# Who copies the transposed attention weights out of PSUM: ScalarE for both heads, or VectorE for the first and ScalarE for the second

## The reference, cut to what matters

```python
z = q @ k.T * scale                       # 128 queries against kv_len keys, per head
log_keep = where(mask, log_sigmoid(-z), 0)
after = cumsum(log_keep, reverse=True) - log_keep
attn = where(mask, exp(log_sigmoid(z) + after), 0)
out = attn @ v
```

## Time and profile before

| | |
|---|---|
| time, median of 3 executions | 1342.16 us (1341.47 to 1343.16) |
| the profiled execution | 1342.95 us, of which its span is 1341.2 us |
| TensorE busy | 1242.6 us, 93% of the span |
| VectorE busy | 468.9 us, 35% |
| ScalarE busy | 381.1 us, 28% |
| GpSimd busy | 121.0 us, 9% |
| mean granted TensorE clock | 0.969 of full speed |

### The profile page before, as it was taken

The page is one execution under the profiler, slowest core; times in us unless marked ns, Lnnn a source line. Parts: engine busy times, 40 slices in busy tenths (PEclk is TensorE's granted clock), DMA queues, the critical chain, the costliest instruction groups (busy, mean ns, idle before and its releaser), DMA issues.

```text
span 1341.2 us, 23288 instructions
## 1 busy us (share of the span) xinstructions
PE 1242.6 (93%) x9734; PEld 602.4 (45%) x9734; DVE 468.9 (35%) x833; ACT 381.1 (28%) x571; POOL 121.0 (9%) x206
## 2 busy tenths in 40 slices
PE   7999999999989999998999956999999999999980
PEld 3444444444557777775445532333333333333320
DVE  3035301244357777774364353111111111111117
ACT  1034402333145565555222122111111111111114
POOL 1000000000021221220000001010101010101010
PEclk9999999999989999999999977999999999999995
DMA  5110001010000001001704019776799499397226
GB/s 220 32 47 31 32 32 47 32 31 16 0 2 3 34 4 34 4 3 65 267 6 157 28 44 354 275 273 197 268 313 312 148 319 367 101 369 254 55 38 259
DMA packets 61013, 170.19 MB, mean 127 GB/s; under 512 B 3184, under 2 KB 3312, under 8 KB 60928
## 3 DMA queue, kind: packets, MB, share of 16 engines
q1 hardware_dynamic: 54384, 145.31, 29.0%
q0 software_dynamic: 6544, 23.63, 7.4%
HBM read 144.29 MB, written 24.64 MB: 126 GB/s over the span
## 4 chain that ended last, share of the span: by engine, by line
PE 84%; DVE 6%; DMA 4%; ACT 3%; issue 2%; POOL 0%; SPq 0%; POOLq 0%; DVEq 0%; ACTq 0%
PE PS L1829 31%; PE PS L205 19%; PE PS L1300 8%; PE PS L214 3%; PE PS L659 3%; PE PS L994 2%; PE PS L678 2%; PE PS L1003 2%; PE PS L1013 2%; PE PS L1822 2%; DMA YT<-x1d,RK 1%; PE PS L348 1%; PE PS L1440 1%; PE PS L734 1%; DMA XS<-in_xT 1%
## 5 line engine op out<-in xcount | busy, mean ns | idle before, releaser
L205 PE MATMUL PS<-XS 128*128 128x512 f32 x672 | 293.9, 597 | 7.6 <-DMA XS<-in_xT 7.1
L1829 PE MATMUL PS<-XS,YT 128*64 128x512 f32 x656 | 287.9, 596 | 3.5 <-DMA SQ<-in_w_upx 2.6
L1829 PE MATMUL PS<-SQ,YT 128*64 128x512 f32 x488 | 216.4, 597 | 0.0
L1829 PE MATMUL PS<-RK,YT 128*64 128x512 f32 x672 | 211.1, 593 | 0.0
L205 PEld LDWEIGHTS PS<-XS 128*128 128x128 f32 x672 | 127.1, 191 | 172.7 <-issue 163.9
L1829 PEld LDWEIGHTS PS<-XS,YT 128*64 128x64 f32 x656 | 88.9, 137 | 185.4 <-issue 180.8
L1300 PE MATMUL PS<-SQ,YT 128*128 128x512 f32 x256 | 114.0, 594 | 0.6 <-issue 0.6
L1917 DVE TENSOR_TENSOR YT<-YT,PS 128x256 f32<-128x256 f32 x42 | 15.8, 418 | 274.7 <-PE PS L1829 274.7
L1829 PEld LDWEIGHTS PS<-RK,YT 128*64 128x64 f32 x672 | 65.9, 137 | 74.7 <-issue 74.7
L1300 PEld LDWEIGHTS PS<-SQ,YT 128*128 128x128 f32 x256 | 47.7, 190 | 56.7 <-issue 56.5
L1829 PEld LDWEIGHTS PS<-SQ,YT 128*64 128x64 f32 x488 | 66.4, 138 | 0.0
(11 more groups left out here) (386 smaller groups left out, 1591.2 us busy)
## 6 DMA issues: line engine op xcount, KB each, us to landing
RK<-in_w_down SPq DMA_DIRECT2D x6, 2048.0 KB, 12.6
XS<-in_w_in SPq DMA_DIRECT2D x21, 512.0 KB, 3.3
XS<-in_w_gate SPq DMA_DIRECT2D x5, 2048.0 KB
XS<-in_w_upx SPq DMA_DIRECT2D x5, 2048.0 KB
XS<-in_w_down SPq DMA_DIRECT2D x5, 2048.0 KB
RK<-in_w_gate SPq DMA_DIRECT2D x5, 2048.0 KB, 19.7
SQ<-in_w_gate SPq DMA_DIRECT2D x4, 2048.0 KB
RK<-in_w_upx SPq DMA_DIRECT2D x4, 2048.0 KB, 19.7
```

The lines of the kernel that those rows point to most:

```text
L205: m = e.matmul(acc[:, half * HB:(half + 1) * HB], XS[:, 8 + n % 4, kt * P:(kt + 1) * P], XS[:, kt, half * HB:(half + 1) * HB], start=kt == ...
L1829: ins = e.matmul(acc[r, :], rows[:, r], third_cols(n, k, at, HB), start=start, stop=stop)
```

## The change

`sba_turned` no longer takes its copy operation from the engine but as an argument. ScalarE calls it in step 2 only, for the second head, and VectorE calls it in step 0, for the first head. Waits, semaphore, source and destination stay as they were.

```diff
-        def sba_turned(e, u, hh):
+        def sba_turned(e, copy, u, hh):
 
             if 0 <= u < NU:
                 w = SPANS[u][4] - SPANS[u][3]
                 wait(e, s_bx, 2 * u + hh + 1)
                 wait(e, s_bv, u - 1)
-                e.copy(AT2[u % 2][:, hh, 0:w], PS[1][:, 0:w]).then_inc(s_bt, 1)
+                copy(AT2[u % 2][:, hh, 0:w], PS[1][:, 0:w]).then_inc(s_bt, 1)
 
         def sba_act(e, j):
             step = j % KINDS
-            if step in (0, 2):
-                sba_turned(e, j // KINDS - 2, step // 2)
+            if step == 2:
+                sba_turned(e, e.copy, j // KINDS - 2, 1)
...
         def sba_dve(e, j):
             step = j % KINDS
+            if step == 0:
+                sba_turned(e, e.tensor_copy, j // KINDS - 2, 0)
```

## The result

| | kernel before | kernel after |
|---|---|---|
| median of 20 executions each, on one chip | 1343.05 us | 1344.91 us |
| lowest and highest | 1337.41 and 1344.25 | 1343.07 and 1348.43 |
| profiled execution, of it the span | 1342.95 us, 1341.2 | 1343.07 us, 1341.3 |
| mean granted TensorE clock | 0.969 | 0.972 |

The times' ratio is 1.0021, with a 95% interval of 1.0012 to 1.0029. The medians lie 1.9 us apart. The ratio over 1, times 1342 us, is 2.8 us, and its interval runs from 1.6 to 3.9. So the kernel is slower by an amount at the edge of what I had called no change (0.2%, 2.7 us). The forecast was 1344.2 us.

What follows compares the result with a forecast made beforehand. TensorE was taken to bound the mixer stage. VectorE's copies, hold less slack place by place, cost 1.97 us, rounded 2.0, and ScalarE's relief gains 0: 1344.2 us against the median of 1342.16, range 1341.0 to 1349.8.

Steps and rivals of the forecast that it cites:

- What bounds the stage: Mixer stage: TensorE sets the pace, busy 236.51 of 250 us; only its 13.5 us of idle time can change.
- The relief at 0: ScalarE's queue: losing 36 copies, 17.5 us of work, gains TensorE 0, at most a single 0.3 us wait.
- What a copy holds up: VectorE's queue: each copy delays the rest by 0.61 us for 512 columns, down to 0.20 for 128; 17.1 us in all.
- place C of block 0: Block 0, 512-column copy: step-2 transposes and the weights L1083 slip, costing 0.60 us for both together.
- place A of block 1: Block 1, 384-column copy: hold 0.48 us less slack 0.05 ahead of TensorE's L659, costing 0.43 us.
- place A of block 4: Block 4, 256-column copy: U ends with slack 0.06 us ahead of TensorE's L659, costing 0.28 us.
- D of block 6: Block 6, 512-column copy: U slips by 0.28 us against slack 0.17 ahead of L774, costing 0.11 us.
- the three small ones: Places in blocks 5, 2 and 3, each under 0.1 us, taken together as 0.15 us.
- the 27: The other copy places, costed at nothing: VectorE idles afterwards for TensorE anyway, or TensorE needs the result later.
- The sum: Mixer stage: hold less slack over the charged places, 1.97 us, rounded to 2.0 us slower.
- The stages behind: Stages behind the mixer: of the same length, so the 2.0 us is expected at the end too.
- VectorE late as a rule: Rival, mixer stage: VectorE's extra 17.1 us makes it late from place to place; 7.6 us slower, 1349.8 us; chance 0.22.

Runs made afterwards that it cites:

- e5: Kernel after, with ScalarE given a dummy copy of the same width in step 0 at 35 of 36 places: 1345.13 us, ratio 1.0025 to the kernel before.
- e4: Kernel before, with ScalarE's first-head copy cut to 8 columns, so the attention's output differs: 1320.84 us, ratio 0.9832.
- e6: Kernel before, with ScalarE's second sigmoid L1049 moved behind its copy L816 in c3 and c9: 1336.62 us against 1341.27, ratio 0.9958.
- e2: Kernel before, with VectorE copying first heads only in the nine spans where the prediction charged a cost: 1344.01 us, ratio 1.0014.
- e1: Kernel before, with VectorE copying first heads only in the 27 spans costed at nothing: 1342.20 us against 1342.12, ratio 1.0001.
- e3: Kernel after, with VectorE copying each first head twice in 35 spans, once into an unused part of TT: 1354.87 us, ratio 1.0101 to the kernel before.
- e7: Kernel after, with ScalarE's second sigmoid L1049 moved behind its copy L816: 1342.90 us, ratio 1.0009 to the kernel before.
- e10: Kernel after, profiled and timed once more without any edit: 1345.54 us, ratio 1.0027 to the kernel before.

## Why the prediction was right, point by point

- **What bounds the stage**: right. TensorE's waits for VectorE grew and ScalarE's lost work did nothing.
- **The relief at 0**: right, shown in three ways. L816 is waited for no less than before (6.8 us against 6.4), e5 gives the work back without a cost, and the mixer stage of e4 gains 0.2 us. The reason given, L1026 stands behind the late L816, is borne out by e6, in which the order alone takes 4.46 us off the middle.
- **What a copy holds up**: right. 0.61, 0.48 and 0.34 were taken for 512, 384 and 256 columns. At place C of block 0 it was 0.59, at place A of block 1 0.45, at place A of block 4 0.32 (the copy started at 510.73, the next row at 511.05). The whole is 17.1 us in the page's busy time, the figure of the working; the "some 20" of the last part was too much. ScalarE's fell by 13.2 on the page, not by 17.5: the copy's rows overlapped those beside them. ScalarE's idle time ahead of copies did not shrink with their number: 34.0 us for the second heads alone, where the earlier trace rows had 30.1 for both heads.
- **The places**: mostly right. D of block 6 did not come (0.11), C of block 0 was 0.11 less, the three small ones 0.09 more. e2 gives 0.83 in the middle where these places had 0.97, and e1 gives 0.14 for the 27 where 0 was taken.
- **The sum**: 1.97 forecast, 1.72 to 1.95 found at the places, 1.9 between the medians and 2.8 by the ratio. What the working did not have is the gap at L795, 1.04 us in the profiled execution (0.73 of it shown as idle time), partly offset by 0.41 elsewhere in the middle. Nothing in the trace of before announces it. That the medians agree with the sum to 0.1 us is therefore in part luck; the terms in the middle were, taken together, somewhat too large (0.97 against 0.63 without the gap, 0.83 in e2).
- **The stages behind**: of the same length within the scatter; in the profiled execution 1.1 us shorter.
- **The chances**: "VectorE late as a rule" at 0.22 was too high beside e1. Its threshold was right in kind, though. With copies made twice (e3) TensorE waits 13 times for the copy, and with ScalarE on time (e7) 9 times for T and U, as that rival said.

## What to carry to other kernels

An engine's total load says little when it is not the bound. A copy costs its hold in the new queue less the slack there, place by place, and it gives back only what waits behind it in the old queue. That slack is borrowed from the waits of others: when those are taken away it has to be read again. Before work is moved to another engine, look at what stands ahead of the late instruction in its own queue, because there moving one piece behind c3 and one behind c9 gave 4.7 us where moving 36 copies cost 2 to 3, and move only the copy with a long idle time ahead of it and urgent work behind it, which was one of 72.

## What was not expected of the hardware

**The clock falls after a short idle time in some executions and not in others.** In block 7 TensorE waits about 1 us for the norm's squares. In some executions the four products L348 behind it then take 3.68 us and in others 1.98, by the same instructions. It isn't the kernel that decides: the kernel after shows 1.98 us in one profile and about 3.3 in the other (e10), with block 7 at 40.85 and 42.47. First e1, then the kernel after:

```profile
614.35 3.68 PE L348 MATMUL PS<-TT,head_ones 128*128 128x512 f32 x4 [1.02 <-ACT TT L1110]
```

```profile
614.82 1.98 PE L348 MATMUL PS<-TT,head_ones 128*128 128x512 f32 x4 [1.01 <-ACT TT L1106]
```

These are the windows from 604 to 630 us of the two, in the same order:

```profile
604.00:630.00 26.00, 22.12 (x404) 13.93 (x396) 12.36 (x21) 13.70 (x22) 0.00 (x0) 0.93 0.04 10
```

```profile
604.00:630.00 26.00, 21.85 (x463) 14.91 (x454) 12.92 (x23) 15.03 (x23) 0.00 (x0) 1.00 0.09 29
```

The granted clock is 0.93 in e1 and 1.00 in the kernel after. 0.07 of 26 us is 1.8 us of full clock lost. By an estimate from these rows that is some 3.6 us at the half level (1.2 GHz instead of 2.4), which is the length of L348. This is the 1.7 us by which block 7 differs in the table (42.3 to 42.5 against 40.7 to 40.9), and with the 0.84 or 0.90 of block 0 it may be a part of the 7 us of scatter between executions of one kernel. Whether a profiled execution has it or not can hide an effect of 2 us. The two equal spans above are a case of block 0's clock: block 7 ran at full clock in both.

**A copy of values can change the time of a later stage.** In e4 the data, and with it the routing, was worth 21 us in a stage that the edit never touched.
